# Transposing x before the final norm at the border of two blocks, with that norm folded into the next one

## What is computed

```python
def _rms_norm(x, g):
    xf = x.astype(jnp.float32)
    y = xf * lax.rsqrt(jnp.mean(xf * xf, axis=-1, keepdims=True) + EPS)
    return (y * g.astype(jnp.float32)).astype(x.dtype)
...
        x = x + _swiglu_ffn(x, ffn_norm[layer], ffn_w_gate_up[layer], ffn_w_down[layer])
    return _rms_norm(x, final_norm)
...
    for l in range(DEPTH):
        h = rms_norm(x, norm_mix_g[l])
        p = h @ w_in[l].astype(h.dtype)
        y_a = conformer_conv(p[..., :CONV_CH], p[..., CONV_CH:o1],
                             conv_w[l], conv_b[l], conv_ln_g[l], conv_ln_b[l])
...
        x = x + y
```

## Time and profile before

| | us |
|---|---|
| median of 3 runs | 1289.65 |
| lowest and highest | 1289.53, 1289.98 |
| the profiled execution's own time | 1289.56 |
| its span | 1287.5 |
| PE busy | 1257.7 |
| DVE busy | 821.8 |
| ACT busy | 673.5 |
| POOL busy | 144.7 |

### The profile page before, as it was taken

The page is one execution under the profiler, slowest core; times in us unless marked ns, Lnnn a source line. Parts: engine busy times, 40 slices in busy tenths (PEclk is TensorE's granted clock), DMA queues, the critical chain, the costliest instruction groups (busy, mean ns, idle before and its releaser), DMA issues.

```text
span 1287.5 us, 16669 instructions
## 1 busy us (share of the span) xinstructions
PE 1257.7 (98%) x6276; PEld 1032.6 (80%) x6276; DVE 821.8 (64%) x953; ACT 673.5 (52%) x806; POOL 144.7 (11%) x169
## 2 busy tenths in 40 slices
PE   7999999999999999999989999999999999999998
PEld 5888888888898678888877778888888877888886
DVE  4466455545567655555459967777746987777763
ACT  6554254434356554444347365766636554776652
POOL 2000000000010000000019610000003931000000
PEclk9999999999999999999999999999999999999999
DMA  8644554446364235545524325444462433544540
GB/s 311 237 157 181 185 195 179 170 177 226 131 245 164 88 130 223 194 172 222 191 101 156 131 98 196 177 158 187 177 225 104 170 116 131 187 171 165 196 180 33
DMA packets 32534, 220.13 MB, mean 171 GB/s; under 512 B 4000, under 2 KB 4032, under 8 KB 6752
## 3 DMA queue, kind: packets, MB, share of 16 engines
q1 hardware_dynamic: 30384, 213.40, 44.9%
q0 software_dynamic: 1664, 5.41, 1.3%
q10 hardware_dynamic: 432, 0.56, 0.1%
HBM read 218.30 MB, written 1.05 MB: 170 GB/s over the span
## 4 chain that ended last, share of the span: by engine, by line
PE 91%; DVE 5%; ACT 2%; issue 1%; POOL 1%; DMA 0%; POOLq 0%; ACTq 0%; DVEq 0%
PE acc L1527 26%; PE acc L1529 26%; PE acc L1528 26%; PE tb L1559 5%; DVE wlo L952 2%; PE acc L1714 1%; PE acc L1716 1%; PE acc L1717 1%; ACT whi L494 1%; DVE cacc L1293 1%; PE tb L1928 1%; PE tb L1628 1%; PE tb L1749 1%; PE tb L1954 0%; PE tb L1768 0%
## 5 line engine op out<-in xcount | busy, mean ns | idle before, releaser
L952 DVE TENSOR_TENSOR wlo<-raw,whi 128x2048 fp32r<-128x2048 f32 x200 | 458.3, 2311 | 235.9 <-ACT whi L494 235.9
L494 ACT ACTIVATE whi<-raw 128x2048 fp32r<-128x2048 f32 x200 | 376.9, 1907 | 109.3 <-PE acc L1529 101.0
L1527 PE MATMUL acc<-whi,xth 128*128 128x512 f32 (+1 forms) x1056 | 420.2, 398 | 7.5 <-DVE xtl L974 4.3
L1529 PE MATMUL acc<-whi,xtl 128*128 128x512 f32 (+1 forms) x1056 | 410.1, 388 | 0.0
L1528 PE MATMUL acc<-wlo,xth 128*128 128x512 f32 (+1 forms) x1056 | 409.3, 388 | 0.0
L1527 PEld LDWEIGHTS acc<-whi,xth 128*128 128x128 f32 x1056 | 199.4, 189 | 54.4 <-issue 8.3
L1529 PEld LDWEIGHTS acc<-whi,xtl 128*128 128x128 f32 x1056 | 199.2, 189 | 41.5
L1528 PEld LDWEIGHTS acc<-wlo,xth 128*128 128x128 f32 x1056 | 199.8, 189 | 37.2
L1527 PE MATMUL acc<-whi,yth 128*128 128x512 f32 x512 | 204.2, 399 | 1.7 <-DVE ytl L1441 1.7
L1529 PE MATMUL acc<-whi,ytl 128*128 128x512 f32 x512 | 200.4, 391 | 0.0
L1528 PE MATMUL acc<-wlo,yth 128*128 128x512 f32 x512 | 200.2, 391 | 0.0
(11 more groups left out here) (239 smaller groups left out, 1018.0 us busy)
## 6 DMA issues: line engine op xcount, KB each, us to landing
raw<-in_stream SPq DMA_DIRECT2D x200, 1024.0 KB, 4.8
rb<-in_rel_rows POOLq DMA_DIRECT2D x8, 256.0 KB, 2.9
raw<-in_stream SPq DMA_DIRECT2D x4, 256.0 KB, 4.9
raw<-in_stream SPq DMA_DIRECT2D x2, 512.0 KB, 6.8
gs_sb<-in_gs_row POOLq DMA_DIRECT2D x1, 1024.0 KB, 5.6
frow<-in_fin_row POOLq DMA_DIRECT2D x2, 512.0 KB, 5.4
x<-in_x_in SPq DMA_DIRECT2D x2, 256.0 KB, 4.1
x<-in_x_in SPq DMA_DIRECT2D x1, 512.0 KB, 8.0
```

The source lines that it names most:

```text
L494: act.activation(whi[:, s, :], raw[:, s, :], ACT.Copy).then_inc(hi_ready, 1)
L952: dve.tensor_tensor(wlo[:, s, :], raw[:, s, :], whi[:, s, :], ALU.subtract).then_inc(lo_ready, 1)
L1527: pe.matmul(o, xh, wh, start=first, stop=False)
L1529: return pe.matmul(o, xl, wh, start=False, stop=last)
```

## The change

The final norm's gain is multiplied into the next norm's gain column once, at the kernel's start (DVE; `gcol` gets a tenth column set, which is a somewhat larger load). At the border x is transposed, gained and split without its final norm, in the order that all other norms have: three quarters' transposes during and right behind the down projection, the fourth inside step 0. `final_root` goes; POOL issues the three small loads, then makes the root of the final norm for both token tiles (`root(FIN1)`), and then the second root, which it multiplies by the first with one more TENSOR_TENSOR. DVE applies the final norm to both tiles of x behind the four `norm_lo`, ahead of `ginl`. ACT takes the final norm's squares behind the four `norm_hi`, and the second norm's squares between `hi(U0 + 2)` and `hi(U0 + 3)`. In layer 0 alone `conv_turn` moves from behind k tile 1 to behind k tile 3 and `logits` from behind 3 to behind 5.

```diff
-        gcol = const("gcol", [9, KT])
+        gcol = const("gcol", [10, KT])
...
-            def root(r):
+            def root(r, outer=None):
...
-                pool.tensor_tensor(stat[:, 2 * r:2 * r + 2], ssq(r, 0, 2), mhalf[:, 0:2], ALU.pow).then_inc(n_r, 1)
+                two = stat[:, 2 * r:2 * r + 2]
+                last = pool.tensor_tensor(two, ssq(r, 0, 2), mhalf[:, 0:2], ALU.pow)
+                if outer is not None:
+                    last.then_inc(x_r2, 1)
+                    pool.wait_ge(x_r2, 1)
+                    last = pool.tensor_tensor(two, two, stat[:, 2 * outer:2 * outer + 2], ALU.mult)
+                last.then_inc(n_r, 1)
...
-            final_root(FIN1, 0)
...
                 pool.dma_start(gin[:, :], gate_in[l]).then_inc(x_ld, 16)
-                root(STATS[4 + 2 * l])
+                if l == 0:
+                    root(FIN1)
+                root(STATS[4 + 2 * l], None if l else FIN1)
...
+            for q in range(4):
+                norm_hi(4, q)
             for m in range(M):
                 square(FIN1, m, n_add, 4 * 3 + 2 * m + 2)
-            norm(4)
-            for m in range(M):
-                square(5, m, f_app, m + 1)
...
                 hi(U0 + 2)
+                if l == 0:
+                    for m in range(M):
+                        square(STATS[4], m, f_app, m + 1)
                 hi(U0 + 3)
...
             dve.wait_ge(gains_loaded, 16)
+            dve.tensor_tensor(gcol[:, 4, :], gcol[:, 4, :], gcol[:, 9, :], ALU.mult).then_inc(f_g, 1)
...
-            add(4, 0)
-            add(4, 1)
-            add(4, 2)
-            apply(FIN1, 0, 0)
-            add(4, 3)
-            norm_gain(4, 0)
-            norm_gain(4, 1)
-            norm_lo(4, 0)
-            norm_lo(4, 1)
-            apply(FIN1, 0, 1)
-            norm_gain(4, 2)
-            norm_gain(4, 3)
-            norm_lo(4, 2)
-            norm_lo(4, 3)
+            dve.wait_ge(f_g, 1)
+            norm(4)
+            dve.wait_ge(n_r, FIN1 + 1)
+            dve.wait_ge(f_row, 16)
+            for m in range(M):
+                dve.wait_ge(n_tr, 4 * 4 + 2 * m + 2)
+                apply(FIN1, m)
...
-                        if j == n - 1 and k not in (4, 8):
+                        if j == n - 1 and k != 8:
...
-            for q in range(2):
-                norm_turn(4, q, f_app, 1)
...
-                                 count=4 * k, mid=last_turn(k) if j == 0 and m == 0 and l else None,
+                                 count=4 * k, mid=last_turn(k) if j == 0 and m == 0 else None,
...
-                step(0, m0={3: second_turns} if l == 0 else {})
+                step(0)
...
-                step(1, m0={1: conv_turn, 3: logits})
+                step(1, m0={1: conv_turn, 3: logits} if l else {3: conv_turn, 5: logits})
```

More of the change, by code:

```diff
@@ L224, in two_blocks_kernel @@
         f_ms, f_rt = sem("final_meaned"), sem("final_rms")
+        f_g, x_r2 = sem("final_gain_folded"), sem("mix_own_rms")
         a_ev, a_vsq, a_vsum, a_ms, a_r, a_vn, a_sp, a_spc, a_y, a_tr, a_hi, a_lo = (
@@ L378, in root @@
                 pool.wait_ge(n_ms, r + 1)
-                pool.tensor_tensor(stat[:, 2 * r:2 * r + 2], ssq(r, 0, 2), mhalf[:, 0:2], ALU.pow).then_inc(n_r, 1)
-            pool.wait_ge(consts_made, 3)
-            def final_root(r, e):
-                for m, (mean, done, n) in enumerate(((f_ms, f_rt, e), (n_ms, n_r, r))):
-                    pool.wait_ge(n_sq, 2 * r + m + 1)
-                    pool.tensor_scalar(ssq(r, m), ssq(r, m), 1.0 / D, EPS, ALU.mult, ALU.add).then_inc(mean, 1)
-                    pool.wait_ge(mean, n + 1)
-                    pool.tensor_tensor(rms(r, m), ssq(r, m), mhalf[:, 0:1], ALU.pow).then_inc(done, 1)
+                two = stat[:, 2 * r:2 * r + 2]
[5 more added lines that the diff above has]
+                last.then_inc(n_r, 1)
+            pool.wait_ge(consts_made, 3)
             root(0)
@@ L477, in _ @@
                         pool.tensor_scalar(a, a, stat[:, 285 + 2 * m:286 + 2 * m], EPS, ALU.add, ALU.add).then_inc(f_ms, 1)
-                        pool.wait_ge(f_ms, m + 2)
+                        pool.wait_ge(f_ms, m + 1)
                         pool.tensor_tensor(rms(FIN2, m), a, mhalf[:, 0:1], ALU.pow).then_inc(f_rt, 1)
@@ L512, in norm @@
                     norm_hi(k, q)
-                if k != 4:
-                    for m in range(M):
-                        square(STATS[k], m, n_add, 4 * (k - 1) + 2 * m + 2)
+                for m in range(M):
+                    square(STATS[k], m, n_add, 4 * (k - 1) + 2 * m + 2)
             def first_hi_quarter(u, i):
@@ L929, in end_scale @@
             def end_scale(m):
-                act.wait_ge(f_rt, m + 2)
+                act.wait_ge(f_rt, m + 1)
                 act.wait_ge(e_xf, 2 * m + 2)
@@ L1229, in _, with apply @@
             glu(1, U_GLU1, 3, PAIR_GLU1)
-            def apply(r, e, m):
-                if m == 0:
-                    dve.wait_ge(f_rt, e + 1)
-                    dve.wait_ge(f_row, 16 * (e + 1))
-                else:
-                    dve.wait_ge(n_r, r + 1)
+            def apply(r, m):
                 dve.scalar_tensor_tensor(x[:, m, :], x[:, m, :], rms(r, m), frow[:, :], ALU.mult,
                                          ALU.mult).then_inc(f_app, 1)
-            add(4, 0)
-            add(4, 1)
-            add(4, 2)
-            apply(FIN1, 0, 0)
-            add(4, 3)
-            norm_gain(4, 0)
-            norm_gain(4, 1)
-            norm_lo(4, 0)
-            norm_lo(4, 1)
-            apply(FIN1, 0, 1)
-            norm_gain(4, 2)
-            norm_gain(4, 3)
-            norm_lo(4, 2)
-            norm_lo(4, 3)
+            dve.wait_ge(f_g, 1)
+            norm(4)
+            dve.wait_ge(n_r, FIN1 + 1)
+            dve.wait_ge(f_row, 16)
+            for m in range(M):
+                dve.wait_ge(n_tr, 4 * 4 + 2 * m + 2)
+                apply(FIN1, m)
             for l in range(2):
@@ L1502, in end_scale @@
             def end_scale(m):
-                dve.wait_ge(f_rt, m + 2)
+                dve.wait_ge(f_rt, m + 1)
                 dve.wait_ge(e_xf, 2 * m + 1)
@@ L1851, in step @@
                             end()
-                def second_turns():
-                    norm_turn(4, 2, f_app, 2)
-                    norm_turn(4, 3)
-                step(0, m0={3: second_turns} if l == 0 else {})
+                step(0)
                 pe.wait_ge(x_gl, l + 1)
@@ L2155 @@
     gains = [A(a_norm)[0], A(ffn_norm)[0], A(kv_norm), A(ffn_norm)[1], A(norm_mix_g_2)[0], A(norm_ffn_g_2)[0],
-             A(norm_mix_g_2)[1], A(b_norm)[0], A(norm_ffn_g_2)[1]]
+             A(norm_mix_g_2)[1], A(b_norm)[0], A(norm_ffn_g_2)[1], A(final_norm)]
     fw, fb = A(ffn_conv_w_2), A(ffn_conv_b_2)
```

## The result

The median fell from 1289.54 us (8 runs, 1287.30 to 1290.86) to **1284.72 us** (8 runs, 1282.72 to 1286.68): a ratio of 0.9963, with the 95% interval 0.9954 to 0.9972. That is 4.8 us less, 0.37%, and more than the 0.2% that the prediction took for the least that can be told from none.

What follows compares the result with a forecast made beforehand. PE bounds the kernel, busy 1257.7 of 1287.5 us. Border 5.09 less 1.38 given back less 0.3 of waiting is 3.4, so 1289.56 becomes 1286.2; forecast 1285.8 to 1286.5 (0.60), range 1285.0 to 1287.5 (0.85).

Steps and rivals of the forecast that it cites:

- The border: First add to gate product takes layer 1's 16.84 us instead of 21.93: 5.09 us gained, 3.54 of it idle time.
- The moved hooks: Layer 0, step 1: two more k tiles ahead of the logits give back 1.38 us; PE waits 1.8 in step 2.
- The full chain behind the logits: DVE's work from the logits to `lo(U0 + 5)` has no slack, so logits 3.71 us early bring everything only 3.7 early.
- Rival 1: Behind the border nothing is given back, the chain behind the logits having slack: 1284.5 us, chance 0.06.
- POOL against DVE: Second root: POOL's small operations collide with DVE's splits, so `conv_turn` waits 0.3 us (ends 0 and 0.9).
- rival 2: Second root: POOL's power is also held to the split's end; wait 0.9, gain 2.8, 1286.8 us, chance 0.15.
- The loads and the first root: At the border POOL's loads delay nothing; the root ends at 662.10 and `ginl` is ready 0.9 us before the gate product.
- rival 3: At the border the first root is late and `ginl` holds up the gate product: gain 2.2 or less, 1287.4 us, chance 0.10.
- rival 5: The wait in step 2 brings the low clock, matmuls 0.43 us apart: slower, up to 1293.4 us, chance 0.04.
- The start: At the kernel's start one more DVE multiplication of 128x8 costs 0 to 0.1 us.
- Rival 4: The border doesn't take layer 1's shape: 0 to 2.5 us gained, 1287.1 to 1289.6, chance 0.05.
- The slow matmuls: At the border PE's matmuls at the lower clock cost 1.55 us, the rest of 5.09 after idle time.

Runs made afterwards that it cites:

- after_split_early: After, with layer 0's split of U0 + 5 directly behind that of U0 + 4 on DVE, and its rounded copy likewise on ACT: 1284.66 us, ratio 0.9964.
- after_logits_up: After, with layer 0's logits directly behind the transposes of `hc`, behind k tile 3 instead of 5: 1284.5 us, ratio 0.9961.
- after_loads_behind: After, with POOL's three small loads behind its first root of the border instead of ahead of it: 1288.85 us, ratio 0.9995.
- the start edit: Before, with only the tenth gain column set loaded and multiplied by DVE at the start, read by nothing: 1289.39 us, ratio 1.0003.
- the third trace of before: Before, unchanged, run once more for another trace of the border: 1288.39 us.
- its two copies: Before, unchanged, run again as two further kernels: 1289.57 us and 1288.39 us.
- before_filled: Before, with 13 matmuls whose result nothing reads, in the two places where PE stands idle at the border: 1287.38 us, ratio 0.9988.

## Why the prediction was right in its steps and low in its gain

**The border: right.** Forecast 5.09, measured 5.08, and the same to 0.03 in all eight traces of kernels that have after's border with the loads ahead of the root. Layer 1's own norm was the right model: the first product behind the border sits where it put it.

**The moved hooks: right in size, wrong in name.** Forecast 1.38 given back and a wait of 1.8 in step 2; measured 1.34 and 1.65. But with the hooks at their old places 1.26 is given back as well. The two k tiles are no price: they stand where a wait for `hc` would stand. The prediction's arithmetic held because the two are of about one size, and that was luck.

**The full chain behind the logits: right.** The brackets are missing in DVE's rows from 673.70 to 725.05, after_split_early only spread the wait, and after_logits_up got 0.33 for 1.40. Rival 1 (nothing given back), whose 1284.5 is closest to the measured time, falls all the same: PE gives the 1.34 back. Its number came out for other reasons.

**POOL against DVE: the operations right, the wait absent.** On the forecast's axis (the trace runs 0.79 early at the gate product) the TENSOR_SCALAR ended at 667.05 (forecast 667.4), the power ran from 667.13 to 667.82 (667.5 to 668.2), the product ended at 670.00 (670.5). The first was held to 0.05 behind its split's end and not 0.2 (in the earlier trace rows too it was less than the prediction read: the first of the two splits there ended at 356.06, the POOL operation at 356.15); the power, half a microsecond ahead of `lo(U0 + 3)`, wasn't held, so rival 2 falls; and `lo(U0 + 3)` took 2.29, not up to 2.82. Half a microsecond was saved over this row of small steps, and the 0.3 at `conv_turn` didn't occur. This is the first mis-sized term.

**The loads and the first root: right.** The loads took POOL 653.04 to 654.7, the root was at 660.30, the gate product waited for nobody: rival 3 falls, and after_loads_behind shows what it guards against. **The clock behind the wait in step 2: right**, 0.24 apart; rival 5 falls. **The start: right**, nothing. Rival 4 fell with the border.

**The slow matmuls: the second mis-sized term.** The step that failed is "and, the rest, 1.55 of slow matmuls": it took one execution's price of the low clock for the kernel's. The clock's part of that execution's border was 1.36, the cheapest of four (against 1.56, 1.62 and, with the start edit, 2.49) and 0.40 below their mean. The change removes the whole of it each time, since after and all its variants show 1.00 there. With the mean the change is worth 5.08 + 0.40 - 1.34 = 4.1 us. The 0.40 rests on four traces: without the one with the start edit it would be 0.15, by the runs' clocks (see the third trace of before) 0.8.

**And the middle of the time.** Before's profiled execution had a cheap border and a dear start and middle, and its 2.06 us around the span were 0.3 more than the 1.75 of before's other runs: the traces of its two copies, of the start edit and of before_filled stand 0.35 to 1.05 ahead of it before the border. Its sum, 1289.56, was nevertheless the median. I set the forecast against that sum, as if each part of it were typical.

Over all runs of this study before has a median of 1289.5 and a mean of 1289.1 (67 runs), after 1284.7 in both (15 runs): 4.8 by the medians, 4.4 give or take 0.7 by the means. The 4.1 from the traces and this agree. Of the 1.5 us between forecast and result, 0.3 is the absent wait, which the rows show. The border's price, which the prediction took as fixed, is shown to vary; its share, 0.4 by the four traces, is an estimate. The other 0.8 or so isn't settled: the start and middle of an execution vary by as much, the border's price may be larger, and by the means only 1.0 us in all has to be explained. The range was too short at its lower end for the same reason: below 1285.8 it held 0.8 us, for a border that gives more, and nothing for what two executions of one kernel differ by.

## What to carry to other kernels

Where a stop of PE is followed by the low clock, the price of the low clock belongs to the execution and not to the kernel: take it from several traces, or fill the stop with dummy matmuls and measure, and widen the range by it. When a gain arrives at an engine with no idle time, look for the whole row of its consumers: taking the first wait away only moves it to the next. A root that is made later than before needs its small inputs issued ahead of it in the same queue; here the order of three loads and one root decided over the whole gain.

## What I had not expected of the hardware

**The granted clock.** At one and the same border, with the same stops, PE stayed at 1.2 GHz for 3.4 us in three traces and for 6.8 in one; the border cost 18.27 to 19.40 us from the down projection's last matmul to the gate product's first, 16.91 with the stops filled. The stretches at the start and at 450 us vary in the same way, in before and after. What the low level costs depends on where it falls: 0.46 to 0.48 us for each us of it in which PE was busy, nothing where PE stood.

**Who is held, POOL or DVE.** After's product of 128x2 began 0.23 behind a split and took 2.11, ending 0.05 behind it; alone it took 0.20. The addition of POOL at 676.06 began 0.06 ahead of a split, kept its 0.74, and the split took 2.83 instead of 2.28. The Trainium skill (SBUF — State Buffer, section "SBUF: two separate sides") says of a GpSimd operation that reads SBUF and a VectorE operation with two SBUF inputs that the one that starts first has the shared ports for its whole instruction and blocks the other. Both rows agree. Two do not: the tap, a TENSOR_SCALAR, that began 0.10 ahead of a split took 3.09 and the split its shortest time, and the power (0.69, a TENSOR_TENSOR of 128x2), still running when `lo(U0 + 3)` began at 666.87, neither lost time nor cost any.

Over all fourteen traces it was POOL's 128x256 additions with two inputs that held a split up: the 108 splits that began 0.06 to 0.27 behind the start of one took 2.82 or 2.83. POOL's operations with one input cost a split at most 0.2: of 88 that began beside a tap 86 took 2.27 or 2.28 and two 2.48, and the 14 that began behind the `kdiag` operation took 2.43 to 2.45. Small operations of DVE do feel a tap, though (0.51 and 0.53 instead of 0.41, above). That the number of inputs is the reason wasn't tried.
